# Attention probabilities: the two halves of each head's band added before the transpose, and separated again behind it

## The chip, the cores and the metric

The kernel runs on one core of a Trainium2 chip. The metric is the device time of one execution in microseconds. TensorE is written PE, VectorE DVE, ScalarE ACT, GpSimd POOL and the DMA-issuing engine SP, as in the profile.

## The reference

A decoder trunk of two layers over 512 tokens of width 1024, all in float32. Layer 0 mixes tokens with an mLSTM, layer 1 with sliding-window attention; each is followed by a gated feed-forward block with a causal convolution. Only the attention of layer 1 matters here, cut from the reference:

```python
diff = qi - (ku - BLK)                       # query in its block, key in [previous block, own block]
band = (diff >= 0) & (diff < WINDOW)         # BLK = WINDOW = 128
s = jnp.where(mask, s, -jnp.inf)
mx = jnp.maximum(jnp.max(s, axis=-1, keepdims=True), sink)
p = jnp.exp(s - mx)
p = p / (jnp.sum(p, axis=-1, keepdims=True) + jnp.exp(sink - mx))
o = jnp.einsum('bnhgqk,bnkhd->bnqhgd', p, vc)
```

There are 16 query heads, two key/value heads and four blocks of 128 queries. Query i of a block sees key j of its own block where j is at most i, and key j of the previous block where j is more than i. So in each row of 256 probabilities exactly 128 can be other than zero, and no column j is used in both halves.

## The kernel before

Matrix products of weights and activations are made three times over in fp32r parts (high times high, low times high, high times low). ACT rounds a weight tile to its high part (`split_hi`, line 564), DVE subtracts it from the raw tile to get the low part (`split_lo`, line 929); PE takes both.

The attention works in 16 steps s (block s // 4, four heads each) and eight pairs m of steps 2m and 2m+1. Each engine has its own written-out queue, and semaphores tie them together. For a step:

- `scores(s)` on PE (line 1834): four matmuls of 128 queries by 256 keys (128 in block 0) into PSUM banks 0 and 1 (odd steps) or 2 and 3 (even steps).
- `masked_max(s)` on DVE (line 1381, small operations at 1387 and 1389): adds the band of 0 and -1e30, takes the row maximum, writes to `sc[:, s % 4]`.
- `probs(s)` on ACT (lines 842 and 844): the exponentials, in place, with their sums.
- `inverse(s)` on DVE (lines 1396 and 1397): adds the sink's term, takes the reciprocal.
- the scaling of `sc` by the reciprocal on POOL (line 545).
- `turn_probs(s)` on PE (line 1847): transposes of 128 by 128, two for each head (one in block 0), all into banks 2 and 3.
- `turned(s)` on ACT (line 851): the copy from PSUM to `p_t[:, s % 2]`.
- `mix(m)` on PE (line 1865): probabilities times values for both steps of a pair, into bank 4; then `mixed_hi` on ACT (line 858) and `mixed_lo` on DVE (line 1404).

PE's queue fills the waits of this chain with other work, `filling(m, 0..3)`: projections in pairs 0 and 1 (lines 1491 to 1493) and, from pair 2, the output projection of an earlier block (lines 1686 to 1688), six matmuls a filling. Other stations of the same queues are `turn` (line 1880, four transposes of the normalised rows), `norm_post` (DVE lines 942 and 945), `norm_pre` (DVE line 958) and `add_bias` (DVE line 952, ACT line 583). DVE also runs the low parts of the output projection's eight weight tiles in this stretch, the last four of them in pair 2. PE's queue in a pair is `scores(2m+3)`, `scores(2m+2)`, `mix(m-1)`, two fillings, `turn_probs(2m)`, a filling, `turn_probs(2m+1)`, the `turn` stations, a filling.

Of the kernel before, what the change touches and what calls it, by code (L numbers as in the profile page):

```python
# [27 lines left out]
ALU = mybir.AluOpType  # L28
ACT = mybir.ActivationFunctionType

P = 128
# [8 lines left out]
def trunk(nc, x, x_turned, columns, m_w_in, m_gate_bias, m_w_out, a_w_in, a_sinks, a_w_out,  # L40
# [3 lines left out]
    KT = D // P  # L44
# [11 lines left out]
    AG = 4  # L56
# [52 lines left out]
    with ExitStack() as ctx:  # L109
# [3 lines left out]
        def sem(name):  # L113
# [75 lines left out]
        sc = arena[:, 22 * KB:38 * KB].rearrange("p (b j k) -> p b j k", b=4, j=AG)  # L189
        p_t = arena[:, 38 * KB:46 * KB].rearrange("p (b j k) -> p b j k", b=2, j=AG)  # L190
        asm = arena[:, 46 * KB:46 * KB + 4 * 6 * AG].rearrange("p (b r j) -> p b r j", b=4, r=6)
        b_out = arena[:, 60 * KB:64 * KB]

        hid = arena[:, 0:44 * KB].rearrange("p (f t) -> p f t", f=FT)
# [60 lines left out]
            sem(n) for n in ("va_mm", "va_done", "s_mm", "mx_done", "p_done", "pt_mm", "pt_done",  # L255
                             "pv_mm", "o_hi", "o_lo"))
        pn_done = sem("pn_done")
        qb_mm = sem("qb_mm")
        t_mm, t_hi, t_lo, inv_done = sem("t_mm"), sem("t_hi"), sem("t_lo"), sem("inv_done")

# [217 lines left out]
        def _(pool):  # L478
# [56 lines left out]
            for n in range(2, 4):  # L535
# [2 lines left out]
                pool.wait_ge(w_lo_done, counted(G_AIN + n - 1))  # L538
                nc.gpsimd.tensor_tensor(w_lo[:, s], raw[:, s % 4], w_hi[:, s].bitcast(F32),
                                        ALU.subtract).then_inc(w_lo_done, 1)  # L540
            for s in range(AT_STEPS):

                b, lo = s % 4, P if s < ASTEPS else 0
                pool.wait_ge(inv_done, s + 1)
                nc.gpsimd.tensor_tensor(sc[:, b, :, lo:], sc[:, b, :, lo:],
                                        asm[:, b, 5].unsqueeze(2).to_broadcast([P, AG, 2 * P - lo]),
                                        ALU.mult).then_inc(pn_done, 1)


        @block.scalar  # L550
        def _(act):
# [293 lines left out]

            def turned(s):

                b, blk = s % 2, s // ASTEPS
                act.wait_ge(pt_mm, s + 1)
                lo = P if blk == 0 else 0  # L850
                nc.scalar.copy(p_t[:, b, :, lo:], ps[:, 2:4].rearrange("p a (j k) -> p (a j) k", k=2 * P)
                               [:, :, lo:]).then_inc(pt_done, 1)

            def mixed_hi(m):

# [24 lines left out]
            for m in range(A_PAIRS):  # L880
                for w in pair_work(m - 1, "turn") + pair_work(m - 1, "post") + pair_work(m, "y"):
                    work(w)
                if m == 0:
                    for k in range(4):
                        split_hi(G_AOUT + k)
                if m == 2:
                    for k in range(4, 6):
                        split_hi(G_AOUT + k)
                if m >= 1:
                    mixed_hi(m - 1)  # L890
                if m == 2:
                    for k in range(6, KT):
                        split_hi(G_AOUT + k)
                for s in (2 * m, 2 * m + 1):
                    turned(s)
                    if s + 2 < AT_STEPS:
                        probs(s + 2)
            for w in pair_work(A_PAIRS - 1, "turn"):
                work(w)
            work(("y", NB - 2))  # L900
# [16 lines left out]
        def _(dve):  # L917
# [474 lines left out]
            def inverse(s):  # L1392
# [3 lines left out]
                link(nc.vector.tensor_tensor(asm[:, b, 4], asm[:, b, 2], asm[:, b, 3], ALU.add))  # L1396
                nc.vector.reciprocal(asm[:, b, 5], asm[:, b, 4]).then_inc(inv_done, 1)

            def mixed_lo(m):

                blk, n = m // 2, m % 2
                dve.wait_ge(o_hi, m + 1)
                at = (slice(None), slice(4 * n, 4 * n + 4), slice(blk * P, (blk + 1) * P))
                nc.vector.tensor_tensor(act_lo[at], ps[:, 4].rearrange("p (t q) -> p t q", t=4),
                                        act_hi[at].bitcast(F32), ALU.subtract).then_inc(o_lo, 1)
# [32 lines left out]
            for m in range(A_PAIRS):  # L1438
                for w in pair_work(m, "y"):
                    work(w)  # L1440
                inverse(2 * m + 1)
                if m + 1 < A_PAIRS:
                    masked_max(2 * m + 2)
                    masked_max(2 * m + 3)
                for w in pair_work(m - 1, "turn"):
                    work(w)
                if m >= 1:
                    mixed_lo(m - 1)
                if m == 0:
                    add_a_bias(6, 1, S // 2, S)  # L1450
                    for k in range(3):
                        split_lo(G_AOUT + k)
                    add_a_bias(7, 1, S // 2, S)
                    split_lo(G_AOUT + 3)
                    gains(2)
                if m == 1:
                    for n in (8, 9):
                        add_a_bias(n, 1, S // 2, S)
                if m == 2:
                    for k in range(4, KT):  # L1460
                        split_lo(G_AOUT + k)
                for w in pair_work(m, "post") + pair_work(m, "pre"):
                    work(w)
                if m + 1 < A_PAIRS:
                    inverse(2 * m + 2)
            for w in pair_work(A_PAIRS - 1, "turn"):
                work(w)
            for w in WORK[AT_STEPS]:
# [16 lines left out]
        def _(pe):  # L1485
# [333 lines left out]
            def scores(s):  # L1819

                blk = s // ASTEPS
                if s % 2:
                    if s >= 3:
                        pe.wait_ge(mx_done, s - 1)
                elif s >= 3:
                    pe.wait_ge(pt_done, s - 2)

                pe.wait_ge(pj_used, QK_UNITS + (6 if s < 2 else A_UNITS if s < 8 else A_UNITS + 4))
                lo = P if blk == 0 else 0
                for j in range(AG):  # L1830
                    _, t, g = pair(s, j)
                    pr = slice(g * DH, (g + 1) * DH)
                    dst = ps[:, score_bank(s) + g, (t % 2) * 2 * P + lo:(t % 2 + 1) * 2 * P]
                    ins = nc.tensor.matmul(dst, q_t[pr, t, blk * P:(blk + 1) * P],  # L1834
                                           k_t[pr, (blk - 1) * P + lo:(blk + 1) * P], start=True, stop=True)
                ins.then_inc(s_mm, 1)

            def turn_probs(s):
                b, blk = s % 4, s // ASTEPS
                pe.wait_ge(pn_done, s + 1)  # L1840
                if s % 2:
                    pe.wait_ge(pt_done, s)
                elif s + 2 < AT_STEPS:
                    pe.wait_ge(mx_done, s + 3)
                for j in range(AG):
                    for kb in range(1 if blk == 0 else 0, 2):
                        ins = nc.tensor.transpose(ps[:, 2 + j // 2, ((j % 2) * 2 + kb) * P:  # L1847
                                                     ((j % 2) * 2 + kb + 1) * P],
                                                  sc[:, b, j, kb * P:(kb + 1) * P], ident[:])
                ins.then_inc(pt_mm, 1)  # L1850

            def mix(m):

                blk = m // 2
                pe.wait_ge(pt_done, 2 * m + 2)
                if m >= 1:
                    pe.wait_ge(o_lo, m)
                else:
# [69 lines left out]
            for m in range(A_PAIRS):  # L1928
# [5 lines left out]
                filling(m, 0)  # L1934
                filling(m, 1)
                turn_probs(2 * m)
                filling(m, 2)
                turn_probs(2 * m + 1)
                for w in pair_work(m, "turn"):
                    work(w)  # L1940
                filling(m, 3)
            mix(A_PAIRS - 1)
            for w in WORK[AT_STEPS]:
# [47 lines left out]
```

## Time and profile before

| | |
|---|---|
| time, median of 3 runs | 1095.64 us (1095.62 to 1095.84) |
| the profiled execution | 1096.03 us, of which the span is 1094.2 us |
| PE busy | 1085.9 us, 99% of the span |
| DVE, ACT, POOL busy | 534.9, 429.0 and 53.7 us |
| granted TensorE clock | 0.999 of full speed |

Times in the rows are counted from the start of the span. A timeline row is: start, duration, engine, line, operation, output<-inputs, count. A run of like instructions is drawn together, and its duration is from the first start to the last end; matmuls overlap, so what one costs is read from start to start.

### The profile page before, as it was taken

To read this page: it belongs to the slowest core of one execution; us is meant where nothing else is said; L and a number is where in the kernel's file an instruction comes from. 1 tells how busy PE (TensorE), PEld (TensorE's weight loads), DVE (VectorE), ACT (ScalarE), POOL (GpSimd) and SP (SyncE) were. 2 spreads that over 40 slices of the span, in tenths; PEclk is the share of its full clock that TensorE was granted. 3 is DMA by queue.
4 is the path that set the end of the run, shared out by engine and by line. 5 is a ranking of instruction groups with operands and counts; after the bars stand their busy time and mean duration, and the time that the engine had idled before them with its cause. 6 is when DMAs were issued, how large, how long until landed. Compare 5 with 4: busy or idle time off the path is not lost.

```text
span 1094.2 us, 14764 instructions
## 1 busy us (share of the span) xinstructions
PE 1085.9 (99%) x5558; PEld 910.8 (83%) x5558; DVE 534.9 (49%) x797; ACT 429.0 (39%) x750; POOL 53.7 (5%) x52
## 2 busy tenths in 40 slices
PE   9999999999999999999999999999999999999997
PEld 7888888898888888888889987789888888888886
DVE  7544578644444434333366587664343434523344
ACT  6511456543232323222355377653333232422242
POOL 1000211000000000000002024200000000000000
PEclk9999999999999999999999999999999999999999
DMA  8342327223323242122272542022323333312231
GB/s 273 107 119 77 116 81 228 72 72 88 114 77 115 77 115 77 39 96 96 96 193 59 153 99 77 2 77 80 113 83 109 87 105 90 101 38 96 96 134 77
DMA packets 141765, 109.51 MB, mean 100 GB/s; under 512 B 22481, under 2 KB 127089, under 8 KB 141729
## 3 DMA queue, kind: packets, MB, share of 16 engines
q1 hardware_dynamic: 140720, 105.84, 32.6%
q0 software_dynamic: 864, 2.92, 0.9%
q8 instruction: 25, 0.41, 0.2%
q10 hardware_dynamic: 144, 0.26, 0.1%
q14 instruction: 12, 0.09, 0.0%
HBM read 106.87 MB, written 2.13 MB: 100 GB/s over the span
## 4 chain that ended last, share of the span: by engine, by line
PE 93%; DVE 3%; ACT 2%; DMA 1%; issue 0%; SPq 0%; POOL 0%; DVEq 0%; ACTq 0%; POOLq 0%
PE ps L1491 17%; PE ps L1492 17%; PE ps L1493 17%; PE ps L1741 7%; PE ps L1742 7%; PE ps L1743 7%; PE ps L1686 3%; PE ps L1688 3%; PE ps L1687 3%; PE ps L1575 1%; PE ps L1577 1%; PE ps L1576 1%; PE ps L1865 1%; PE ps L1847 1%; PE ps L1834 1%; PE ps L1641 1%
## 5 line engine op out<-in xcount | busy, mean ns | idle before, releaser
L1491 PE MATMUL ps<-act_hi,w_hi 128*128 128x512 f32 (+1 forms) x1016 | 368.3, 363 | 0.1
L1492 PE MATMUL ps<-act_lo,w_hi 128*128 128x512 f32 (+1 forms) x1016 | 366.4, 361 | 0.0
L1493 PE MATMUL ps<-act_hi,w_lo 128*128 128x512 f32 (+1 forms) x1016 | 366.4, 361 | 0.0
L1491 PEld LDWEIGHTS ps<-act_hi,w_hi 128*128 128x128 f32 x1016 | 191.7, 189 | 31.2 <-DVE w_lo L929 0.9
L1493 PEld LDWEIGHTS ps<-act_hi,w_lo 128*128 128x128 f32 x1016 | 191.7, 189 | 28.9
L1492 PEld LDWEIGHTS ps<-act_lo,w_hi 128*128 128x128 f32 x1016 | 191.8, 189 | 28.8
L1741 PE MATMUL ps<-w_hi 128*128 128x512 f32 x288 | 112.0, 389 | 0.0
L1742 PE MATMUL ps<-w_lo,w_hi 128*128 128x512 f32 x288 | 112.0, 389 | 0.0
L1743 PE MATMUL ps<-w_hi,w_lo 128*128 128x512 f32 x288 | 112.0, 389 | 0.0
L757 ACT ACTIVATE arena<-ps,vecs 128x512 f32<-128x512 f32 x44 | 34.3, 779 | 188.6 <-PE ps L1493 188.6
L1257 DVE SCALAR_TENSOR_TENSOR arena<-ps,vecs,arena 128x511 f32<-128x511 f32 x44 | 33.0, 749 | 144.5 <-ACT arena L757 144.4
L751 ACT CAST w_hi<-raw 128x1024 fp32r<-128x1024 f32 x80 | 83.1, 1044 | 39.4 <-PE ps L1493 39.4
L1291 DVE TENSOR_TENSOR w_lo<-raw,w_hi 128x1024 fp32r<-128x1024 f32 x32 | 39.2, 1225 | 119.9 <-ACT w_hi L782 119.9
L1249 DVE TENSOR_TENSOR w_lo<-raw,w_hi 128x1024 fp32r<-128x1024 f32 x80 | 94.1, 1217 | 0.2
L564 ACT CAST w_hi<-raw 128x1024 fp32r<-128x1024 f32 x66 | 67.9, 1045 | 64.2 <-PE ps L1577 24.7
L1266 DVE TENSOR_TENSOR arena<-ps,arena 128x512 f32 (+1 forms) x44 | 30.4, 692 | 117.1 <-PE ps L1493 113.5
L929 DVE TENSOR_TENSOR w_lo<-raw,w_hi 128x1024 fp32r<-128x1024 f32 x64 | 76.9, 1219 | 17.8 <-ACT w_hi L564 17.7
L782 ACT CAST w_hi<-raw 128x1024 fp32r<-128x1024 f32 x32 | 33.8, 1055 | 129.1 <-PE ps L1743 129.1
L1743 PEld LDWEIGHTS ps<-w_hi,w_lo 128*128 128x128 f32 x288 | 54.1, 188 | 11.3
L1741 PEld LDWEIGHTS ps<-w_hi 128*128 128x128 f32 x288 | 54.1, 188 | 11.3
L1742 PEld LDWEIGHTS ps<-w_lo,w_hi 128*128 128x128 f32 x288 | 54.1, 188 | 11.0
L761 ACT ACTIVATE arena<-arena 128x512 f32<-128x512 f32 x44 | 27.8, 632 | 79.6 <-DVE arena L1261 79.6
(210 smaller groups left out, 1224.3 us busy)
## 6 DMA issues: line engine op xcount, KB each, us to landing
raw<-in_f_w_up SPq DMA_DIRECT2D x88, 512.0 KB, 4.7
raw<-in_f_w_down SPq DMA_DIRECT2D x44, 512.0 KB, 3.2
raw<-in_m_w_in SPq DMA_DIRECT2D x23, 512.0 KB, 4.5
raw<-in_m_w_out SPq DMA_DIRECT2D x8, 512.0 KB, 3.2
raw<-in_a_w_in SPq DMA_DIRECT2D x16, 256.0 KB, 4.4
raw<-in_a_w_out SPq DMA_DIRECT2D x16, 256.0 KB, 4.8
h<-in_x SPq DMA_DIRECT2D x4, 512.0 KB, 7.4
h<-in_x_turned SPq DMA_DIRECT2D x3, 512.0 KB, 7.9
```

The source lines that it names most:

```text
L564: nc.scalar.copy(w_hi[:, s], raw[:, s % 4]).then_inc(w_hi_done, 1)
L751: nc.scalar.copy(w_hi[:, 4 + s], raw[:, s]).then_inc(w_hi_done, 1)
L757: nc.scalar.activation(cv[:, t], ps[:, 2 * t], ACT.Identity, scale=taps[l][:, 2, bass.ds(f, 1)], bias=taps[l][:, 3, bass.ds(f, 1)]).then_i ...
L929: nc.vector.tensor_tensor(w_lo[:, s], raw[:, s % 4], w_hi[:, s].bitcast(F32), ALU.subtract).then_inc(w_lo_done, 1)
L1249: nc.vector.tensor_tensor(w_lo[:, 4 + s], raw[:, s], w_hi[:, 4 + s].bitcast(F32), ALU.subtract).then_inc(w_lo_done, 1)
L1291: nc.vector.tensor_tensor(w_lo[:, j], raw[:, j], w_hi[:, j].bitcast(F32), ALU.subtract).then_inc(w_lo_done, 1)
L1491: nc.tensor.matmul(dst, uh[:, k], zh, start=(k == 0), stop=False)
L1492: nc.tensor.matmul(dst, uh[:, k], zl, start=False, stop=False)
L1493: ins = nc.tensor.matmul(dst, ul[:, k], zh, start=False, stop=(k == KT - 1))
L1741: nc.tensor.matmul(dst, hi[:, bs], w_hi[:, s, hs], start=start, stop=False)
L1742: nc.tensor.matmul(dst, hi[:, bs], w_lo[:, s, hs], start=False, stop=False)
L1743: return nc.tensor.matmul(dst, lo[:, bs], w_hi[:, s, hs], start=False, stop=stop)
```

## The change

It changes how the probabilities of blocks 1 to 3 (steps 4 to 15) get turned. POOL's `fold(s)` adds the previous block's half of a head's row onto its own block's half and then scales the 128 sums; PE turns 128 columns a head, four transposes a step instead of eight; ACT's copy, now 128x512, gives the previous block's part of `p_t`, and POOL multiplies that part by a mask (`keep_prev`); DVE reads the same PSUM bank a second time, masks it with `causal` (which holds 0 where a key is allowed) and writes the own block's part (`keep_own`). Each step of a pair gets a PSUM bank of its own, bank 2 or 3. The stations are reordered: both `turn_probs` stand together ahead of the third filling, ACT makes `probs(2m+2)` ahead of `turned(2m)` and `turned(2m+1)`, and in pair 2 DVE's four weight splits are put before, between and behind the new stations. In block 0 only this order changes. The mask `prev_keys` is made once by POOL, ahead of the first step. The diff:

```diff
+            nc.gpsimd.memset(prev_keys, 1.0).then_inc(pool_done, 1)
+            pool.wait_ge(pool_done, 10)
+            nc.gpsimd.affine_select(out=prev_keys, in_=prev_keys, compare_op=ALU.is_gt, fill=0.0, base=0,
+                                    pattern=[[-1, P]], channel_multiplier=1).then_inc(pool_done, 1)
+            pool.wait_ge(pool_done, 11)
+            def fold(s):
+                b = s % 4
                 pool.wait_ge(inv_done, s + 1)
-                nc.gpsimd.tensor_tensor(sc[:, b, :, lo:], sc[:, b, :, lo:],
-                                        asm[:, b, 5].unsqueeze(2).to_broadcast([P, AG, 2 * P - lo]),
+                own = sc[:, b, :, P:]
+                if s >= ASTEPS:
+                    nc.gpsimd.tensor_tensor(own, own, sc[:, b, :, 0:P], ALU.add).then_inc(pf_done, 1)
+                    pool.wait_ge(pf_done, s - ASTEPS + 1)
+                nc.gpsimd.tensor_tensor(own, own, asm[:, b, 5].unsqueeze(2).to_broadcast([P, AG, P]),
                                         ALU.mult).then_inc(pn_done, 1)
+            def keep_prev(s):
+                pool.wait_ge(pt_done, s + 1)
+                part = p_t[:, s % 2, :, 0:P]
+                nc.gpsimd.tensor_tensor(part, part, prev_keys.unsqueeze(1).to_broadcast([P, AG, P]),
+                                        ALU.mult).then_inc(prev_done, 1)
+            for m in range(A_PAIRS):
+                for s in (2 * m, 2 * m + 1):
+                    fold(s)
+                if 2 * m >= ASTEPS:
+                    for s in (2 * m, 2 * m + 1):
+                        keep_prev(s)
...
             def turned(s):
-                b, blk = s % 2, s // ASTEPS
+                part = slice(P, 2 * P) if s < ASTEPS else slice(0, P)
                 act.wait_ge(pt_mm, s + 1)
-                lo = P if blk == 0 else 0
-                nc.scalar.copy(p_t[:, b, :, lo:], ps[:, 2:4].rearrange("p a (j k) -> p (a j) k", k=2 * P)
-                               [:, :, lo:]).then_inc(pt_done, 1)
+                nc.scalar.copy(p_t[:, s % 2, :, part], ps[:, 2 + s % 2].rearrange("p (j k) -> p j k", j=AG))\
+                    .then_inc(pt_done, 1)
...
+                if m + 1 < A_PAIRS:
+                    probs(2 * m + 2)
                 for s in (2 * m, 2 * m + 1):
                     turned(s)
-                    if s + 2 < AT_STEPS:
-                        probs(s + 2)
+                if m + 1 < A_PAIRS:
+                    probs(2 * m + 3)
...
+            def keep_own(s):
+                dve.wait_ge(pt_done, s + 1)
+                nc.vector.scalar_tensor_tensor(p_t[:, s % 2, :, P:], causal[:].unsqueeze(1).to_broadcast([P, AG, P]),
+                                               0.0, ps[:, 2 + s % 2].rearrange("p (j k) -> p j k", j=AG),
+                                               ALU.is_equal, ALU.mult).then_inc(own_done, 1)
...
                 if m == 2:
-                    for k in range(4, KT):
-                        split_lo(G_AOUT + k)
+                    split_lo(G_AOUT + 4)
                 for w in pair_work(m, "post") + pair_work(m, "pre"):
                     work(w)
+                if 2 * m >= ASTEPS:
+                    for s in (2 * m, 2 * m + 1):
+                        keep_own(s)
+                if m == 2:
+                    split_lo(G_AOUT + 5)
                 if m + 1 < A_PAIRS:
                     inverse(2 * m + 2)
+                if m == 2:
+                    for k in range(6, KT):
+                        split_lo(G_AOUT + k)
...
                 if s % 2:
                     if s >= 3:
                         pe.wait_ge(mx_done, s - 1)
+                elif s >= 2 * ASTEPS:
+                    pe.wait_ge(own_done, s - 2 - ASTEPS)
                 elif s >= 3:
                     pe.wait_ge(pt_done, s - 2)
...
             def turn_probs(s):
                 pe.wait_ge(pn_done, s + 1)
-                if s % 2:
-                    pe.wait_ge(pt_done, s)
-                elif s + 2 < AT_STEPS:
+                if s % 2 == 0 and s + 2 < AT_STEPS:
                     pe.wait_ge(mx_done, s + 3)
                 for j in range(AG):
-                    for kb in range(1 if blk == 0 else 0, 2):
-                        ins = nc.tensor.transpose(ps[:, 2 + j // 2, ((j % 2) * 2 + kb) * P:
-                                                     ((j % 2) * 2 + kb + 1) * P],
-                                                  sc[:, b, j, kb * P:(kb + 1) * P], ident[:])
+                    ins = nc.tensor.transpose(ps[:, 2 + s % 2, j * P:(j + 1) * P], sc[:, b, j, P:], ident[:])
                 ins.then_inc(pt_mm, 1)
             def mix(m):
                 blk = m // 2
-                pe.wait_ge(pt_done, 2 * m + 2)
+                if blk == 0:
+                    pe.wait_ge(pt_done, 2 * m + 2)
+                else:
+                    pe.wait_ge(own_done, 2 * m + 2 - ASTEPS)
+                    pe.wait_ge(prev_done, 2 * m + 2 - ASTEPS)
...
                 turn_probs(2 * m)
-                filling(m, 2)
                 turn_probs(2 * m + 1)
                 for w in pair_work(m, "turn"):
                     work(w)
+                filling(m, 2)
                 filling(m, 3)
```

## Rows read from the trace of the kernel before

**Rows 1.** The page, busy time and share of the span.

```profile
PE 1085.9 (99%) x5558; PEld 910.8 (83%) x5558; DVE 534.9 (49%) x797; ACT 429.0 (39%) x750; POOL 53.7 (5%) x52
```

**Rows 2.** Busy time by stretch: PE, PEld, DVE, ACT, POOL, granted clock, DMA.

```profile
628.00:720.00 92.00, 91.75 (x614) 72.41 (x613) 64.15 (x207) 63.30 (x183) 26.80 (x16) 1.00 0.22 56
```

**Rows 3.** Waits in the stretch 628 to 720: total, times, longest.

```profile
PE ps L1847 <- ACT arena L851: 0.3, 1, 0.3
```

**Rows 4.** Timeline of PE, pairs 0, 2, 3 and 4.

```profile
632.18 0.60 PE L1847 MATMUL ps<-ident,arena 128*128 128x128 f32 x4
632.53 0.37 PE L1491 MATMUL ps<-act_hi,w_hi 128*128 128x256 f32 x1
...
633.92 0.28 PE L1493 MATMUL ps<-act_hi,w_lo 128*128 128x256 f32 x1
634.45 0.63 PE L1847 MATMUL ps<-ident,arena 128*128 128x128 f32 x4 [0.25 <-ACT arena L851]
...
652.01 1.04 PE L1847 MATMUL ps<-ident,arena 128*128 128x128 f32 x8
652.80 0.49 PE L1686 MATMUL ps<-w_hi,act_hi 128*128 128x512 f32 x1
653.12 0.40 PE L1687 MATMUL ps<-w_lo,act_hi 128*128 128x512 f32 x1
653.36 0.40 PE L1688 MATMUL ps<-w_hi,act_lo 128*128 128x512 f32 x1
...
656.63 2.00 PE L1834 MATMUL ps<-arena 64*128 64x256 f32 x16
...
663.30 1.04 PE L1847 MATMUL ps<-ident,arena 128*128 128x128 f32 x8
...
667.92 2.00 PE L1834 MATMUL ps<-arena 64*128 64x256 f32 x16
```

**Rows 5.** Timeline of ACT: the smaller copy, then an exponential step.

```profile
643.01 0.59 ACT L851 COPY arena<-ps 128x512 f32<-128x512 f32 x1 [2.91 <-PE ps L1847]
...
676.58 0.51 ACT L842 ACTIVATE arena<-arena 128x256 f32<-128x256 f32 x1
...
678.65 0.99 ACT L851 COPY arena<-ps 128x1024 f32<-128x1024 f32 x1
```

**Rows 6.** Groups of POOL by line and shape: busy, mean ns of one.

```profile
L539 POOL TENSOR_TENSOR w_lo<-raw,w_hi 128x1024 fp32r<-128x1024 f32 x2 | 5.7, 2830 | 410.3 <-ACT w_hi L564 410.3
...
L545 POOL TENSOR_TENSOR arena<-arena 128x512 f32<-128x512 f32 x4 | 4.1, 1040 | 49.1 <-DVE arena L1397 49.1
L533 POOL TENSOR_TENSOR arena<-arena,h 128x512 f32<-128x512 f32 x3 | 3.8, 1268 | 0.0
```

**Rows 7.** Timeline of DVE, pairs 2 to 4.

```profile
653.74 4.62 DVE L929 TENSOR_TENSOR w_lo<-raw,w_hi 128x1024 fp32r<-128x1024 f32 x4
...
659.16 1.47 DVE L1396 TENSOR_TENSOR arena<-arena 128x4 f32<-128x4 f32 x1 [0.52 <-ACT arena L844]
...
660.79 0.48 DVE L1381 CUSTOM_DVE_ANT_0 arena<-ps,band,sink 128x256 f32<-128x256 f32 x1
...
664.71 0.68 DVE L1404 TENSOR_TENSOR act_lo<-ps,act_hi 128x512 fp32r<-128x512 f32 x1
...
668.03 1.22 DVE L952 TENSOR_TENSOR arena<-ps,arena 128x1024 f32<-128x1024 f32 x1 [0.17 <-PE ps L1688]
...
675.30 1.27 DVE L942 SCALAR_TENSOR_TENSOR arena<-arena,stat,g_post 128x1024 f32<-128x1024 f32 x1
676.61 1.22 DVE L945 TENSOR_TENSOR h<-h,arena 128x1024 f32<-128x1024 f32 x1
```

**Rows 8.** Timeline of POOL in pairs 2 to 4.

```profile
658.72 1.89 POOL L545 TENSOR_TENSOR arena<-arena 128x1024 f32<-128x1024 f32 x1 [7.47 <-DVE arena L1397]
...
667.94 1.89 POOL L545 TENSOR_TENSOR arena<-arena 128x1024 f32<-128x1024 f32 x1 [5.12 <-DVE arena L1397]
```

**Rows 9.** Timeline of POOL and DVE where both work, 576 to 588.

```profile
577.91 2.40 POOL L539 TENSOR_TENSOR w_lo<-raw,w_hi 128x1024 fp32r<-128x1024 f32 x1 [406.44 <-ACT w_hi L564]
578.37 3.02 DVE L945 TENSOR_TENSOR h<-h,arena 128x1024 f32<-128x1024 f32 x1
```

More of the change, by code:

```diff
@@ L191, in trunk @@
         asm = arena[:, 46 * KB:46 * KB + 4 * 6 * AG].rearrange("p (b r j) -> p b r j", b=4, r=6)
+        prev_keys = arena[:, 46 * KB + P:46 * KB + 2 * P]
         b_out = arena[:, 60 * KB:64 * KB]
@@ L257, in trunk @@
         pn_done = sem("pn_done")
+        pf_done, own_done, prev_done = sem("pf_done"), sem("own_done"), sem("prev_done")
         qb_mm = sem("qb_mm")
@@ L540, in _ @@
                                         ALU.subtract).then_inc(w_lo_done, 1)
-            for s in range(AT_STEPS):
-                b, lo = s % 4, P if s < ASTEPS else 0
-                pool.wait_ge(inv_done, s + 1)
-                nc.gpsimd.tensor_tensor(sc[:, b, :, lo:], sc[:, b, :, lo:],
-                                        asm[:, b, 5].unsqueeze(2).to_broadcast([P, AG, 2 * P - lo]),
-                                        ALU.mult).then_inc(pn_done, 1)
+            nc.gpsimd.memset(prev_keys, 1.0).then_inc(pool_done, 1)
[5 more added lines that the diff above has]
+                b = s % 4
+                pool.wait_ge(inv_done, s + 1)
+                own = sc[:, b, :, P:]
[3 more added lines that the diff above has]
+                nc.gpsimd.tensor_tensor(own, own, asm[:, b, 5].unsqueeze(2).to_broadcast([P, AG, P]),
+                                        ALU.mult).then_inc(pn_done, 1)
+            def keep_prev(s):
[9 more added lines that the diff above has]
+                        keep_prev(s)
         @block.scalar
```

## The prediction

> **What bounds the kernel now.** I read the page first, then the busy time by stretch, then the waits and timelines of the attention. PE is busy 99% of the span [rows 1]. In the 92 us of attention it is busy 91.75 us at the full clock, granted 1.00, so 2.4 GHz [rows 2], and the one wait the trace charges to PE in the transposes is 0.3 us [rows 3]. So the attention costs what PE's own instructions cost, start to start. Work taken off PE is time won, one for one, as long as nothing that PE then waits for is late. DVE and ACT have about 28 us free there and POOL 65 us, but free time on average is not free time in the chain. The reader should look at how early each result lands before PE asks for it: that is all this change has to spend.
>
> **What it removes.** Eight transposes take 0.79 us until the next matmul starts, four take 0.35 [rows 4]. Twelve steps lose four each: 12 x 0.44 = 5.3 us, 0.11 us a transpose. The duration of one transpose in isolation is no guide. The Trainium skill ("TensorE: Matmul & The Clock Gate", Part 4: PE-mode transpose) gives some 275 ns for one within a kernel and says that transposes don't count as busy for the clock; at that figure the 48 would be an estimated 13 us. The rows show them pipelined, at the full clock, so the rows' price stands.
>
> With both groups of transposes together, one change from transposes back to matmuls goes in each of the eight pairs: the first matmul then takes 0.32 instead of 0.24 us [rows 4], some 0.1 us with the change in the other direction: 0.8 us in all. In pair 0 the second group no longer waits for the copy: it started 0.53 us after the last matmul where 0.12 is usual [rows 4]: 0.4 us. Together 6.5 us if nothing is late.
>
> **What it adds, and the lock.** ACT copies 512 columns a step, not 1024 (0.6 against 1.0 us) [rows 5]: a gain on ACT, which isn't the bound. DVE gets two `keep_own` a pair; the nearest row, a PSUM operation of 512 columns, takes 0.68 us [rows 7]: 1.34 a pair. POOL had 1.89 us a step [rows 8]. The new scaling of 512 is the 1.04 us row. The add and `keep_prev` read two full streams, like the 1.27 us row, and 2.40 for 1024 in rows 9 fits it; the bounds are 1.04 and 1.27, and I take 1.27 [rows 6, 9]. A fold is then 1.27 + 0.08 + 1.04 = 2.4 us, with `keep_prev` 3.7 us a step, 7.3 a pair of about 10.4 us.
>
> POOL and DVE also exclude each other. A DVE add of 4 columns took 1.47 us and ended with POOL's instruction, at 660.62 [rows 7, 8]; DVE's add of two SBUF tensors of 1024 took 3.02 us instead of 1.22 because POOL was busy until 580.31, and it ended 1.08 us after that, so a handover hides about 0.14 us [rows 9]. A DVE operation with an operand in PSUM goes through beside POOL: 1.22 us at 668.03 [rows 7, 8]. So `keep_own`, `masked_max`'s large part and `mixed_lo` go free; the weight splits, both parts of `norm_post`, `norm_pre` and the small adds at 1387 and 1396 take turns with POOL, a whole instruction at a time. The Trainium skill ("SBUF — State Buffer", SBUF: two separate sides) calls this an exclusive lock, held for a whole instruction; a later section (A bandwidth-pool intuition that's wrong) has a blocked party go on some 115 ns after the release. By that figure each handover would cost, not hide, and pair 3 below would be an estimated 1.2 us later.
>
> **Where it gets late: pair 2 into pair 3.** PE's queue. Pairs 0 and 1 bring the transposes of pair 2 from 652.01 to about 651.4. Then 0.79 for both groups, 2.86 for two fillings, 0.09: scores of pair 3 at 655.1, and by the old distance (663.30 - 656.63 = 6.67) [rows 4] PE asks for step 6 at 661.8 and for step 7 at 662.25.
>
> DVE's queue. `masked_max` of steps 6 and 7 starts when the scores end, about 647.7, takes 3.9 us (660.79 to 664.71) [rows 7] and is held up by POOL's folds for 0.7 in the small add: 652.3. `mixed_lo` 0.6, the first split 1.14 (a quarter of 4.54) [rows 7]: 654.0. ACT's copy of step 4 comes at 653.7, because `probs(6)` (2.07 us) [rows 5] now stands ahead of it. From 654.0 POOL and DVE pass one lock: two `keep_prev` 2.54, three splits 3.4, `inverse(6)` 0.4, two folds 4.8; 11.1 us, less five handovers of 0.14: 664.5. Step 7's fold can't be earlier, since `inverse(7)` stands behind the last split. Behind it wait the transposes of step 7, the fillings and the next scores. PE loses 664.5 - 662.25 = 2.3 us. Bounds: 0 if the lock weren't there (DVE alone would be through at 659.5, POOL at 662); 1.4 at 1.04 us for add and mask; 3.0 with no overlap at handovers.
>
> **Pairs 4 to 7.** Let S be the start of a pair's scores. The transposes come at S + 6.67 as before, the next scores at S + 11.29 - 0.96 = S + 10.3 [rows 4]. DVE's `masked_max` ends at S + 2.07 + 3.9 = S + 6.0, plus 0 to 1.1 for small adds behind the longer folds; I take 0.5. `mixed_lo` ends at S + 7.1.
> - Pair 4: `norm_post`'s first half (1.3) [rows 7] ends at S + 8.4, `keep_prev(8)`, waiting since S + 7.9, takes the lock until 9.5, the second half ends at 10.6, both `keep_own` at 12.0. Before, nothing stood behind `norm_post` that PE needed soon; now the even scores of the next pair wait for `keep_own`, which reads their banks 2 and 3, and `keep_own` stands behind it on DVE. The second scores of the next pair are due at 11.3: 0.7 us late (0 to 1.4).
> - Pair 5: `norm_pre` (1.3) ends at S + 8.4, and `turn`, which now comes right behind the transposes at S + 7.55, waits for it: 0.9 us (0.1 to 1.5).
> - Pair 6: as pair 4 with one `turn` part more (0.6 us) on DVE: `keep_own` ends at S + 12.6. `mix(6)` needs it and comes at S + 10.8 (no scores stand before it): 1.8 us (0.5 to 2.5).
> - Pair 7: the two folds end at S(6) + 17.8, the last transposes are due at 17.85: nothing, 0.5 at most.
>
> Sum of the new waits: 2.3 + 0.7 + 0.9 + 1.8 = 5.7 us; bounds 0.6 (without the lock) and 8.9. Behind the attention PE isn't made to wait, and the DMAs of the next layer's weights are early; what is won or lost stays. The net is 6.5 - 5.7 = 0.8 us won. Against the profiled execution, 1096.03 us (span 1094.2 and 1.8 around it), that is 1095.2; against the median of the runs, 0.4 lower, 1094.8 us.
>
> **The rivals.**
> - *The cover holds.* The waits come out near their lower bounds, because POOL's instructions slip in between DVE's without holding up the ones that matter, or because add and mask take 1.04 us. For it: POOL is idle 65 of 92 us, and each wait above depends on an order at the lock which I chose. Against it: in pair 3 all of the serial work lies before the last fold, whatever the order. With waits of about 1.5 to 3 us, 3.5 to 5 are won: 1091.4 (1090.5 to 1093).
> - *The lock costs more and pair 3 decides*: slower. In pair 3 the transposes of step 7 need `fold(7)`, behind four lock holders of DVE and seven of POOL; if no handover hides anything (3.0, or 4.2 by the figure of the skill above) and pairs 4 to 6 come at their upper bounds, waits are 8.9 to 10 us: 1098.5. It decides from waits of 8.7 us on. For it: `masked_max(8)`, which the transposes of step 6 wait for, ended only 0.5 us before they began already, and then has POOL's folds beside it.
> - *PE's clock falls in the new waits.* Then matmuls behind a wait run at the lower level. The rows show 1.00 all through, with no wait of 2 us to judge by; some us more. It goes into the slower share.
> - *Nothing is won since PE wasn't the limit.* Rows 2 and 3 exclude it.
>
> **How the numbers follow.** This kernel's measurement tells 0.2%, 2.2 us, from no change. My forecast, waits of 4.3 to 8.7 us against 6.5 won, has 0.47: 1093.5 to 1097.8. The cover holds: 0.37. More than 8.7 us, or the clock: 0.16. The range for 8 in 10 leaves out the ends of both rivals: 1090.8 to 1097.3; the likeliest case's own is 1093.5 to 1097.3.
>
> **What the profile would show.** Transposes x8 in one run a pair, 0.79 us to the next matmul; POOL's add and mask near 1.27 us; DVE's `keep_own` near 0.7; weight splits and line 945 longer than 1.22 us, where POOL holds the lock. PE's waits: in pair 3 ahead of the transposes, about 2.3 us on POOL; ahead of the scores or `mix` in pairs 5 and 7 on DVE; ahead of `turn` in pair 5 on DVE. I am wrong if POOL and DVE run side by side, if PE's wait in pair 3 is under 1 us, or if a wait shows up where I have none, on ACT for example, whose copy now stands behind `probs`.

## The result, and the profile after

| | before | after |
|---|---|---|
| median of 17 runs each | 1095.84 us (1095.38 to 1096.63) | 1097.91 us (1096.40 to 1099.07) |
| ratio | | 1.0018, interval 1.0011 to 1.0025 |
| profiled execution, span | 1096.03, 1094.2 us | 1098.43, 1096.7 us |

The change makes the kernel 2 us slower. That is within the 0.2% which the prediction called no change, its likeliest case, but 0.6 us above the upper end of its range and 3.1 us above its 1094.8. It also lies just beyond the 1097.8 us at which that case ended, and since PE's clock fell, as shown below, it belongs by its mechanism to the slower share, which had 0.16.

The page of the kernel after, then the attention's stretch: it answers to [rows 1, 2].

```profile
PE 1083.0 (99%) x5510; PEld 907.4 (83%) x5510; DVE 548.0 (50%) x809; ACT 424.9 (39%) x750; POOL 82.4 (8%) x78
```

```profile
628.00:720.00 92.00, 86.10 (x555) 66.85 (x555) 75.53 (x218) 57.84 (x180) 54.00 (x40) 0.98 0.22 56
```

PE has 48 instructions fewer, and it is busy 86.1 of 92 us where it was busy 91.75: it waits now. POOL's work in the stretch has doubled, DVE's is up by 11 us. The granted clock is 0.98 on average, no longer 1.00. Who PE waits for in the kernel after (total, times, longest):

```profile
PE ps L1886 <- DVE arena L1415: 2.4, 1, 2.4
...
PE ps L1906 <- DVE arena L1428: 1.1, 1, 1.1
PE ps L1921 <- DVE arena L984: 0.9, 1, 0.9
PE ps L1886 <- POOL arena L557: 0.6, 1, 0.6
PE ps L1876 <- DVE arena L1428: 0.6, 1, 0.6
PE ps L1906 <- issue: 0.3, 1, 0.3
```

Lines have moved: 1876 is `scores`, 1886 `turn_probs`, 1906 `mix`, 1921 `turn`, 1415 the end of `masked_max`, 1428 `keep_own`, 984 `norm_pre`, 555 the add and 557 the scaling in `fold`, 564 `keep_prev`, 955 `split_lo`, 1413 the small add in `masked_max`, 1422 the one in `inverse`, 971 the second half of `norm_post`, 1726 to 1728 the output projection. A wait marked "issue" has no releaser that the profile shows. Where these waits lie, in PE's timeline:

```profile
651.73 1.03 PE L1886 MATMUL ps<-ident,arena 128*128 128x128 f32 x8
652.52 0.49 PE L1726 MATMUL ps<-w_hi,act_hi 128*128 128x512 f32 x1
...
655.48 2.00 PE L1876 MATMUL ps<-arena 64*128 64x256 f32 x16
657.80 1.95 PE L1906 MATMUL ps<-arena 128*64 128x256 f32 x16 [0.32 <-issue]
...
662.30 0.39 PE L1728 MATMUL ps<-w_hi,act_lo 128*128 128x512 f32 x1
665.10 1.26 PE L1886 MATMUL ps<-ident,arena 128*128 128x128 f32 x8 [2.41 <-DVE arena L1415]
666.01 0.77 PE L1726 MATMUL ps<-w_hi,act_hi 128*128 128x512 f32 x1
...
670.43 2.00 PE L1876 MATMUL ps<-arena 64*128 64x256 f32 x16
...
682.56 1.14 PE L1876 MATMUL ps<-arena 64*128 64x256 f32 x8 [0.60 <-DVE arena L1428]
...
690.33 0.66 PE L1921 MATMUL ps<-ident,arena 128*128 128x128 f32 x4 [0.89 <-DVE arena L984]
...
705.63 1.95 PE L1906 MATMUL ps<-arena 128*64 128x256 f32 x16 [1.05 <-DVE arena L1428]
...
711.63 0.66 PE L1886 MATMUL ps<-ident,arena 128*128 128x128 f32 x4 [0.62 <-POOL arena L557]
```

Read from start to start, so that the drain around each wait counts: pair 3's transposes come at 665.10 instead of 662.53, 2.6 us; pair 3's `mix` 0.4; pair 5's scores 0.9 and `turn` 1.1; pair 7's `mix` 1.1 and its second transposes 0.8. That is 6.9 us. But from 665.10 to the next scores at 670.43 pass 5.33 us, where the same work takes 3.73 in pair 4: 1.6 us more. The clock shows why, in the stretches of the kernel after around this wait (third from the end: the granted clock):

```profile
662.50:665.10 2.60, 0.19 (x2) 0.03 (x1) 2.57 (x11) 0.12 (x1) 2.28 (x2) 1.00 0.93 270
665.10:667.00 1.90, 1.90 (x10) 1.72 (x11) 1.87 (x11) 1.90 (x9) 0.00 (x0) 0.69 1.20 296
667.00:669.10 2.10, 2.10 (x6) 1.65 (x5) 1.84 (x5) 2.10 (x9) 1.40 (x2) 0.50 0.58 144
669.10:671.00 1.90, 1.90 (x12) 1.32 (x12) 0.59 (x2) 1.09 (x6) 1.90 (x2) 0.96 0.00 0
```

PE had stood idle for 2.41 us (the bracket in its row; the 2.6 us are counted from start to start). Some 0.7 us after it began again its clock fell to 0.50, the lower level of 1.2 GHz, for about 3.4 us (worked out from the granted shares of the three last stretches), and a matmul of 512 columns then took 0.43 us from start to start instead of 0.23. Waits and clock together are 8.5 us lost, against 5.9 won: from pair 0's scores to the last `mix`, PE needs 86.42 us (629.00 to 715.42) where it needed 83.76 (628.84 to 712.60).

What holds pair 3 up is in the timelines of DVE, then POOL, of the kernel after:

```profile
653.03 1.22 DVE L955 TENSOR_TENSOR w_lo<-raw,w_hi 128x1024 fp32r<-128x1024 f32 x1
654.16 1.28 DVE L1428 SCALAR_TENSOR_TENSOR arena<-causal,ps 128x512 f32<-128x512 f32 x2
655.36 1.22 DVE L955 TENSOR_TENSOR w_lo<-raw,w_hi 128x1024 fp32r<-128x1024 f32 x1
656.49 1.23 DVE L1422 TENSOR_TENSOR arena<-arena 128x4 f32<-128x4 f32 x1
...
657.85 3.41 DVE L955 TENSOR_TENSOR w_lo<-raw,w_hi 128x1024 fp32r<-128x1024 f32 x2
661.18 0.99 DVE L1422 TENSOR_TENSOR arena<-arena 128x4 f32<-128x4 f32 x1
...
664.07 0.80 DVE L1413 TENSOR_TENSOR arena<-sink,arena 128x4 f32<-128x4 f32 x1
664.79 0.15 DVE L1415 TENSOR_SCALAR arena<-arena 128x4 f32<-128x4 f32 x1
```

```profile
654.08 3.62 POOL L564 TENSOR_TENSOR arena<-arena 128x512 f32<-128x512 f32 x2 [2.42 <-ACT arena L875]
658.01 2.16 POOL L555 TENSOR_TENSOR arena<-arena 128x512 f32<-128x512 f32 x1 [0.31 <-DVE arena L1423]
660.25 1.90 POOL L557 TENSOR_TENSOR arena<-arena 128x512 f32<-128x512 f32 x1
662.47 1.27 POOL L555 TENSOR_TENSOR arena<-arena 128x512 f32<-128x512 f32 x1 [0.31 <-DVE arena L1423]
663.81 1.04 POOL L557 TENSOR_TENSOR arena<-arena 128x512 f32<-128x512 f32 x1
```

Read them side by side. POOL's add takes 1.27 us alone and 2.16 behind a split; the two splits behind `inverse(6)` take 3.41 us, 2.3 alone; three adds of four columns take 1.23, 0.99 and 0.80 us, each ending with a POOL instruction. The two engines hand one resource to and fro, as in [rows 7 to 9]. In pairs 4 and 6 it is `norm_post`'s second half that is held up:

```profile
679.10 2.21 DVE L971 TENSOR_TENSOR h<-h,arena 128x1024 f32<-128x1024 f32 x1
```

### The profile page after: what moved, and what is told of

Read it like the earlier page. It is cut to its first block, busy times and chain, and to the rows that moved or that the text cites. A ratio compares the mean times of both kernels' runs of the same rounds, so it can differ in the third digit from the quotient of the medians.

```text
span 1096.7 us, 14699 instructions
## 1 busy us (share of the span) xinstructions
PE 1083.0 (99%) x5510; PEld 907.4 (83%) x5510; DVE 548.0 (50%) x809; ACT 424.9 (39%) x750; POOL 82.4 (8%) x78
## 4 chain that ended last, share of the span: by engine, by line
PE 90%; DVE 6%; ACT 2%; issue 1%; POOL 1%; DVEq 0%; ACTq 0%; POOLq 0%
PE ps L1531 18%; PE ps L1532 17%; PE ps L1533 17%; PE ps L1783 7%; PE ps L1781 7%; PE ps L1782 7%; PE ps L1726 2%; PE ps L1728 2%; PE ps L1727 2%; DVE arena L1407 1%; PE ps L1615 1%; PE ps L1617 1%; PE ps L1616 1%; DVE h L971 1%; PE ps L1876 1%; PE ps L1681 1%
```

## The experiments

Ten kernels; a ratio is to the kernel before, run on the same chip. The kernel after stands at 1.0018 on this scale. It was measured in one set of runs only, and the kernel before took 1095.84 to 1096.23 us in the different sets, so a difference to the kernel after carries up to 0.4 us of that.

### What the transposes are worth: `e1_own_half_only`

```diff
-                if s >= ASTEPS:
-                    nc.gpsimd.tensor_tensor(own, own, sc[:, b, :, 0:P], ALU.add).then_inc(pf_done, 1)
-                    pool.wait_ge(pf_done, s - ASTEPS + 1)
...
-                        keep_prev(s)
...
-                        keep_own(s)
...
-                    pe.wait_ge(own_done, 2 * m + 2 - ASTEPS)
-                    pe.wait_ge(prev_done, 2 * m + 2 - ASTEPS)
+                pe.wait_ge(pt_done, 2 * m + 2)
```

> The kernel after, in its new order, without POOL's add, without keep_prev and without keep_own: the previous block's half of the probabilities is left out of the sum and the own block's half of p_t is not written; mix runs all its matmuls. So PE's instructions are those of the kernel after and nothing is added on POOL or DVE. If my price for the transposes and the changes between kinds of work is right (5.3 + 0.8 + 0.4 us), this is 6.5 us under the kernel before, ratio 0.994, and PE waits for nothing in the attention. Rival: the new order alone makes waits, or transposes cost less than 0.11 us each; then under 4 us are won.

1089.86 us, ratio 0.9944 (0.9930 to 0.9958): 6.2 us under the kernel before. The profile lists no wait of PE in the attention; from start to start some 0.3 us are lost ahead of pair 5's `turn`. From pair 0's scores to the last `mix` the profiled execution needs 78.17 us where the kernel before needs 83.76: 5.6 us won, 5.9 with the 0.3. The medians say 6.2 and 6.5; the profiled execution was the slowest of its five, 0.6 us above their median. So the removed work is worth 5.9 to 6.5 us, and the whole 8 us up to the kernel after are what the additions do.

### The clock: `e2_pe_kept_busy`

```diff
                 filling(m, 1)
+                if m == 3:
+                    keep_warm(22)
                 turn_probs(2 * m)
```

> The kernel after with 22 transposes of the identity into the unused bank 5 put before the transposes of step 6, about 2.4 us at 0.11 us each, in the place of PE's wait of 2.6 us. The output is not touched. If the half clock that followed that wait in the trace (granted 0.50 for some 4 us, worth 1.6 us) comes from PE's standing still, it stays at 1.00 here and the time falls by 1.6 us against the kernel after, to about 1096.3. Rival: it comes from something else, or transposes do not keep the clock up; then the time is that of the kernel after, 1097.9, or more.

1096.76 us, ratio 1.0007 (0.9998 to 1.0016); its profiled span is 2.0 us under that of the kernel after. The DVE and POOL queues run as before, and every other wait of PE is there (0.7, 0.9, 1.1, 0.6 us). The clock stays up, in the stretches that answer to the fall above:

```profile
660.00:664.00 4.00, 4.00 (x29) 3.59 (x28) 3.93 (x12) 0.00 (x0) 3.61 (x3) 1.00 0.87 248
664.00:668.00 4.00, 3.99 (x25) 3.31 (x23) 3.73 (x15) 3.56 (x14) 1.14 (x2) 1.00 1.00 263
```

The mean granted clock of each execution, which is measured to 0.001, says the same: 0.999 or 1.000 in all eleven with the transposes, 0.998 in 14 of the 17 of the kernel after (3.4 us at half the clock take 0.0016 off the mean). So PE's standing still brings the clock down, and 22 transposes that compute nothing hold it. They hold it although the Trainium skill ("TensorE: Matmul & The Clock Gate", Part 4: PE-mode transpose) says that transposes don't count as busy in the same way: here the measurement decides against the skill. In the medians the effect is 1.2 us, not 1.6. The kernel after scatters over 2.7 us where the kernel before scatters over 1.3, and its three fastest executions, 1096.4 to 1097.0 us, are the three with a mean clock of 0.999 or 1.000: the fall doesn't come in every execution. More on this below, at `e6_no_keep_own`.

### The serial work: `e3_splits_later`

```diff
                     masked_max(2 * m + 2)
+                if m == 3:
+                    for k in range(6, KT):
+                        split_lo(G_AOUT + k)
...
                     inverse(2 * m + 2)
-                if m == 2:
-                    for k in range(6, KT):
-                        split_lo(G_AOUT + k)
```

> The kernel after with the last two of DVE's weight splits moved from the end of pair 2 to pair 3, behind masked_max(8). If pair 3's wait comes from the serial work of DVE and POOL ahead of masked_max(8) and fold(7), it shrinks from 2.6 us to under 0.7 and the clock does not fall: 4 us less than the kernel after, about 1094. Rival: the wait only moves to the third filling of pair 3, which needs the last split, or to step 7's transposes; then less than 1.5 us are won.

1096.34 us, ratio 1.0002 (0.9993 to 1.0011): 1.6 us won against the kernel after, not 4. PE's waits in this kernel:

```profile
PE ps L1887 <- POOL arena L557: 1.2, 2, 0.6
...
PE ps L1727 <- DVE w_lo L955: 0.5, 1, 0.5
```

The 2.6 us in one piece are gone, and with it the fall of the clock, but 0.55 us for `fold(7)` and 0.5 us for the moved splits take its place: the two splits took 4.30 us there, 2.3 alone, since POOL ran its second fold and `keep_prev` beside them. From start to start PE loses 0.7, 0.8 and, at pair 4's scores, 0.4 us: 1.9 us in three pieces instead of 2.6 in one. The profiled span is 2.3 us shorter, 0.7 by the waits and 1.6 by the clock, so most of what this order won is the clock. My theory was half right, the rival half. As the output projection's wait stands, for two weight tiles at a time, both splits must be done ahead of the third filling.

### Lock or DVE's own work: `e4_masks_on_dve`, `e5_no_keep_prev`, `e6_no_keep_own`

In the first, DVE makes both masks from PSUM:

```diff
             def keep_own(s):
-                dve.wait_ge(pt_done, s + 1)
+                dve.wait_ge(pt_mm, s + 1)
+                nc.vector.tensor_tensor(p_t[:, s % 2, :, 0:P], ps[:, 2 + s % 2].rearrange("p (j k) -> p j k", j=AG),
+                                        prev_keys.unsqueeze(1).to_broadcast([P, AG, P]),
+                                        ALU.mult)
...
-                        keep_prev(s)
```

> The kernel after with the previous block's mask made by DVE too, straight from PSUM (12 more DVE operations of some 0.6 us), so that ACT's copy and POOL's keep_prev fall away in blocks 1 to 3. If turn-taking of POOL and DVE is the cost, 15 us of POOL's lock are gone for 7 us on DVE that need no lock, and the time is 1 to 3 us under the kernel after. If DVE's own added work is the cost, it doubles and the time is 1 to 3 us over the kernel after.

1098.71 us, ratio 1.0023 (1.0014 to 1.0033): not told apart from the kernel after, neither theory's number. The waits are pair 3's 2.6 us as before, and 1.6 us instead of 1.1 at pair 7's `mix`:

```profile
PE ps L1888 <- DVE arena L1414: 2.6, 1, 2.6
...
PE ps L1907 <- DVE arena L1430: 1.6, 1, 1.6
```

The lock does give time back: `inverse(6)`'s small add takes 0.16 us instead of 1.23, and in pairs 4 and 6 `norm_post`'s second half takes 1.23 us instead of 2.21. But 0.6 us more a step in DVE's own queue takes it away. The exchange is even, so DVE's own work isn't free either. The other two leave out one mask each:

```diff
-                if 2 * m >= ASTEPS:
-                    for s in (2 * m, 2 * m + 1):
-                        keep_prev(s)
...
-                    pe.wait_ge(prev_done, 2 * m + 2 - ASTEPS)
+                    pe.wait_ge(pt_done, 2 * m + 2)
```

> The kernel after without POOL's keep_prev: the previous block's part of p_t keeps the whole folded row, so its mask is left out. DVE's work is untouched. If POOL and DVE take turns, 2.5 us of held lock are gone in every pair: pair 3's wait shrinks from 2.6 us to under 0.5 and the clock stays up, norm_post's second half is no longer held up, and 4 to 6 us are won against the kernel after: 1092 to 1094. If DVE's own added work makes PE wait, less than 1 us is won.

```diff
-                if 2 * m >= ASTEPS:
-                    for s in (2 * m, 2 * m + 1):
-                        keep_own(s)
...
-                elif s >= 2 * ASTEPS:
-                    pe.wait_ge(own_done, s - 2 - ASTEPS)
...
-                    pe.wait_ge(own_done, 2 * m + 2 - ASTEPS)
```

> The kernel after without DVE's keep_own: the own block's part of p_t is not written, and scores and mix no longer wait for it. POOL's work is untouched. If DVE's own added work makes PE wait, nearly everything comes back: 7 us or more against the kernel after, about 1090. If the lock has a share of its own, POOL's keep_prev still holds up the splits and inverse(6), pair 3's wait stays at 1 us or more, and the gain is 4 to 6 us: 1092 to 1094.

Without `keep_prev`: 1093.01 us, ratio 0.9973 (0.9962 to 0.9983), 4.9 us under the kernel after. Without `keep_own`: 1096.73 us, ratio 1.0004 (0.9995 to 1.0013), only 1.5 us under it. Leaving out POOL's mask, which no DVE instruction waits for by a semaphore, gives back three times what leaving out DVE's own mask does. These are not shares of one sum: with `keep_prev` gone, `keep_own` and POOL's add still cost 3.2 us against `e1_own_half_only`, and no run leaves out the add alone. The first row is `norm_post`'s second half in the kernel without `keep_prev`, the second in the kernel without `keep_own` (mean ns behind the busy time):

```profile
L968 DVE TENSOR_TENSOR h<-h,arena 128x1024 f32<-128x1024 f32 x3 | 3.7, 1224 | 0.1
```

```profile
L971 DVE TENSOR_TENSOR h<-h,arena 128x1024 f32<-128x1024 f32 x3 | 5.6, 1879 | 0.1
```

PE's waits without `keep_prev`, then without `keep_own`:

```profile
PE ps L1883 <- DVE arena L1412: 1.7, 1, 1.7
PE ps L1883 <- POOL arena L557: 0.7, 1, 0.7
```

```profile
PE ps L1881 <- DVE arena L1415: 2.5, 1, 2.5
...
PE ps L1900 <- POOL arena L564: 1.2, 2, 1.0
PE ps L1915 <- DVE arena L984: 1.0, 1, 1.0
```

`inverse(6)`'s small add, which took 1.23 us in the kernel after, takes in the kernel without `keep_prev`:

```profile
656.57 0.15 DVE L1419 TENSOR_TENSOR arena<-arena 128x4 f32<-128x4 f32 x1
```

So `keep_prev` makes most of the waits of pairs 5 and 7 at scores, `turn` and `mix`, and 0.7 us of pair 3's. The expectation missed in one thing: 1.7 us stay in pair 3, not 0.5, because splits, the small adds and the folds still take turns there. And without `keep_own` PE waits for `keep_prev` in its stead.

The times without `keep_own` lie in two groups, 4 between 1095.2 and 1095.6 and 7 between 1096.6 and 1097.6, about 1.7 us apart, near the price of one fall of the clock. Its profiled execution is of the lower group, 1095.25 us, and there the clock stayed at 1.00 behind a wait of 2.46 us, where 2.41 us in the kernel after and 2.58 us in `e4_masks_on_dve` had brought it down:

```profile
662.00:666.00 4.00, 1.61 (x12) 1.51 (x13) 3.93 (x20) 1.73 (x7) 2.07 (x2) 1.00 1.08 295
666.00:670.00 4.00, 4.00 (x26) 2.96 (x24) 2.69 (x7) 3.97 (x15) 3.01 (x3) 1.00 0.37 91
```

A wait of this length brings the clock down in some executions and not in others. The mean granted clock of each execution bears this out in `e4_masks_on_dve`: seven executions at 0.997 or 0.998 take 1098.5 to 1099.8 us, four at 0.999 take 1097.4 to 1098.1. Without `keep_own` it doesn't part the groups so well, 0.997 or 0.998 in the upper, 0.998 to 1.000 in the lower (the kernel before, where nothing falls, shows 0.998 now and then too), and no execution of the upper group has a timeline: that the clock fell there is an inference.

### Other orders: `e7_reordered_a`, `e8_reordered_b`

Of the edit, beside the two splits that move as in `e3_splits_later` (`keep_owns` makes both `keep_own` of a pair):

```diff
...
+                if pair_work(m, "post"):
+                    _, b = pair_work(m, "post")[0]
+                    norm_post(2 * NB + b, b, 6, biased=True, between=keep_owns)
...
                 turn_probs(2 * m)
+                if m == 7:
+                    filling(m, 2)
                 turn_probs(2 * m + 1)
+                if m == 5:
+                    filling(m, 2)
                 for w in pair_work(m, "turn"):
                     work(w)
-                filling(m, 2)
+                if m not in (5, 7):
+                    filling(m, 2)
```

> The kernel after with four stations moved: the last two weight splits behind masked_max(8) as in the run with later splits; keep_own between the two halves of norm_post in pairs 4 and 6; turn behind the third filling in pair 5; the third filling between the two groups of transposes in pair 7. Each wait that the trace of the later splits showed in pairs 5 to 7 (0.5, 0.9, 1.1 and 0.6 us) should fall to near nothing, 0.2 us go to two more changes of PE's work: some 3 us under the run with later splits, 1093.4, below the kernel before too. Rival: waits move on to the next station, and less than 1 us is won.

1092.80 us, ratio 0.9971 (0.9960 to 0.9982), 3.5 us under the later splits alone. The waits at pair 5's scores, at `turn` and at pair 7's `mix` are gone. Left are pair 3's 0.55 and 0.5 us, 0.4 at pair 4's scores (from start to start), and some 0.3 each at pair 3's `mix`, at pair 7's second transposes and at the last `mix`. The second order keeps the stations of `keep_own`, `turn` and the fillings. Its splits and the projection's wait, against the kernel after:

```diff
                     masked_max(2 * m + 3)
+                if m == 3:
+                    split_lo(G_AOUT + 7)
...
                 if m == 2:
-                    for k in range(6, KT):
-                        split_lo(G_AOUT + k)
+                    split_lo(G_AOUT + 6)
...
-                    pe.wait_ge(w_lo_done, counted(G_AOUT + 2 * q + 1))
+                    pe.wait_ge(w_lo_done, counted(G_AOUT + max(ks or [2 * q + 1])))
```

> As the reordered kernel a, but split 6 stays in pair 2, split 7 goes behind masked_max(9), and the output projection waits for each weight tile by itself. If pair 3's remaining waits (0.6, 0.5, 0.5 us) come from both splits standing together, another 0.5 to 1 us is won: 1092.6. If split 6 in pair 2 makes masked_max(8) late again, it is 0.5 to 1 us slower than a.

1092.76 us, ratio 0.9969 (0.9957 to 0.9981): the same as a. Pair 3's waits fell as expected, from 0.55 and 0.5 to one of 0.3 us, and pair 4's scores come on time, but pair 7's `mix` waited 0.7 us in its profile; neither the gain nor the loss that was expected can be told in the medians.

### Without the mask of the previous block: `e9_value_difference`, `e10_value_difference_reordered`

A folded row times the previous block's values, plus its own block's masked part times (own values less previous values), is the same sum, and needs no `keep_prev`:

```diff
...
+            pool.wait_ge(va_done, 1)
+            nc.gpsimd.tensor_tensor(vd, va[:, 1:NB], va[:, 0:NB - 1], ALU.subtract).then_inc(prev_done, 1)
...
-                        keep_prev(s)
...
+                            values_of = vd[:, blk - 1, gs] if blk and kb else va[:, blk - 1 + kb, gs]
-                            ins = nc.tensor.matmul(ps[gs, 4, 2 * n * P:(2 * n + 2) * P], va[:, blk - 1 + kb, gs],
+                            ins = nc.tensor.matmul(ps[gs, 4, 2 * n * P:(2 * n + 2) * P], values_of,
```

> The kernel after, but the previous block's part stays unmasked: mix multiplies the whole folded row with the previous block's values and the own block's masked part with the difference of the two blocks' values, made once by POOL. The sum is the same as the reference's, and keep_prev is gone for one more POOL instruction. If what counts is POOL's hold on the lock behind the transposes, this takes the time of the run without keep_prev, 1093.0. Rival: that run was fast for another reason, or the subtraction comes late for mix; then more than 1094.

1092.49 us, ratio 0.9968 (0.9956 to 0.9981), as without `keep_prev`. The last kernel adds the later split 7 of b, with its wait for each weight tile by itself, and the third filling between pair 7's transposes:

> As the value difference, and with split 6 left in pair 2, split 7 behind masked_max(9), a wait of the output projection for each weight tile by itself, and pair 7's third filling between its two groups of transposes. The trace without keep_prev shows two waits of PE, 1.7 us in pair 3 and 0.65 in pair 7; with both gone and 0.1 us for one more change of work, 1090.8, 0.5% under the kernel before. Rival: pair 3's wait stays, because masked_max(8) still stands behind inverse(7) and the folds; then 1092 or more.

1090.44 us, ratio 0.9949 (0.9935 to 0.9963): 5.5 us under the kernel before, 7.5 under the kernel after, and the fastest complete version of all. The profile lists no wait of PE in the attention (from start to start it takes 0.5 us more than in `e1_own_half_only`); the whole list lies before it:

```profile
PE ps L1536 <- POOL ident L485: 1.9, 1, 1.9
PE ps L1529 <- DVE arena L972: 0.3, 1, 0.3
```

## Why the prediction was right or wrong

- **The price of the removed work** (6.5 us): right in kind, in part counted twice. The row of eight transposes still takes 0.79 us to the next matmul, and it now holds two steps. I took 0.35 us for each step, so 0.70 a pair, and then counted one change of work less on top, 0.1 a pair; but the difference of 0.79 and 0.70 is nearly that change. Six pairs at 0.79 + 0.1 and pair 0's 0.5 give 5.8 us, and pair 1, where only this change was to be won, takes 9.74 us from scores to scores before and after. The rows of `e1_own_half_only` say 5.9 with its wait of 0.3, its median 6.5; that the median agrees with my sum to a tenth is luck in part. The 13 us that the 275 ns of the Trainium skill ("TensorE: Matmul & The Clock Gate", Part 4: PE-mode transpose) would give are excluded.
- **The durations of what is added**: right. POOL's add 1.27 us, scaling 1.04, `keep_own` 0.68 where nothing is in the way; the upper of my two bounds for the add was the true one.
- **Turn-taking of POOL and DVE**: right. `e5_no_keep_prev` shows it in the durations of DVE's instructions (2.21 us back to 1.22, 1.23 back to 0.15) and in the time, 4.9 us. What DVE's added work costs by itself isn't settled: 1.5 us came back without `keep_own`, but there PE waits for `keep_prev` instead, and `e4_masks_on_dve` shows that it counts.
- **Pair 3** (2.3 us): right in size and cause, 2.6 us. I had the last fold as the one that PE waits for; it was `masked_max(8)`, at 664.94, with `fold(7)` through at 664.85. Both stand behind the same serial work. `e3_splits_later` shows that moving both splits doesn't bring both in time; with split 7 alone moved, a wait for each weight tile and no `keep_prev` (`e10_value_difference_reordered`) PE waits for neither.
- **Pairs 5 to 7**: scores 0.7 predicted, 0.9 measured; `turn` 0.9 and 1.1; pair 7's `mix` 1.8 and 1.1, since the small adds were held up less than I took. Pair 7's transposes, predicted at nothing with 0.5 us as the most, lost 0.8: POOL's last scaling took 1.90 us instead of 1.04 behind `norm_pre`, which I hadn't set against it. Pair 3's `mix` lost 0.4 that I hadn't looked for: `keep_prev(5)`, held up by a split, came late. In sum, with pair 3's transposes, 5.7 predicted, 6.9 measured. Waits where I had none were one of my signs of being wrong.
- **The step that failed**: "PE's clock falls in the new waits ... some us more. It goes into the slower share." I had named the mechanism and given it no term in the sum. It cost 1.6 us in the profiled execution and 1.2 in the medians (`e2_pe_kept_busy`), since 14 of 17 executions have it and three seem not to. The rows close the sum: 5.9 won, 6.9 of waits and 1.6 of clock make 2.6 us lost, and the attention takes 2.7 us more. Against my 0.8 us won that is 1.6 for the clock, 1.2 for the waits (the two missed ones in pairs 3 and 7 are as much) and 0.6 for the price. My rows had no PE wait of this length to price it by; the price of the lower level itself, twice the time of a matmul for as long as it lasts, could have bounded it.
- Two slips in the text: with 3.0 us as the bound, the 115 ns of the Trainium skill ("SBUF — State Buffer", A bandwidth-pool intuition that's wrong) at five handovers give an estimated 3.6 us, not 4.2, and in pair 3 an estimated 1.3 us more, not 1.2. The skill's figure isn't borne out here: with POOL's instruction from 663.81 to 664.85, the add of four columns waiting for it was through at 664.87.

## What to carry to other kernels

When PE is the bound and work is moved off it, cost the helpers' queues by what they hold and who stands behind them, not by their free time: here POOL had 65 us to spare and its 15 us of masks cost 5. An operation of DVE with an operand in PSUM goes beside POOL, one with two SBUF operands doesn't, so place those where nobody is close behind. One wait of PE of 2.4 us or more was dearer here than nearly the same time in several pieces, because the clock can fall behind it. And sometimes algebra (the difference of the values) removes the helper that no order tried here could hide.

## What the runs showed of the hardware

- PE's clock fell to the lower level after stops of 2.41 us (kernel after) and 2.58 us (`e4_masks_on_dve`) inside dense work, and stayed there for about 3.4 us in both; after a stop of 2.46 us (`e6_no_keep_own`) it did not. After waits of 1.7 us and less in the attention it stayed up in each profile here.
- Transposes of the identity in the place of such a stop kept the clock at 1.00 in the profile, and at 0.999 or more on average in all eleven executions (`e2_pe_kept_busy`).
- A DVE instruction on four columns can take 1.2 us when POOL is at work, and POOL's 1.04 us can become 1.90. The loss shows in the duration of the row, not as a wait.
